# Attention heads with values stationary in column halves, and two head pairs' work interleaved

## What is computed

```python
s = einsum('bqhd,bkhd->bhqk', qn, k_nope) + einsum('bqhr,bkr->bhqk', qp, k_pe)
p = softmax(s.astype(float32) * scale, axis=-1)
o = einsum('bhqk,bkhd->bqhd', p, v)          # then o @ wo
```

## Time and profile before

| | |
|---|---|
| three runs | 3949.35, 3950.53 (median), 3956.2 us |
| profiled execution | span 3955.7 us; the page gives no other time for it |
| TensorE busy | 3625.6 us (92%), mean granted clock 0.956 |
| VectorE, ScalarE, GpSimd busy | 2466.1 (62%), 938.1 (24%), 1840.3 us (47%) |
| chain that ended last | TensorE 71%, VectorE 16%, issue 3%, ScalarE 3% |

### The profile page before, as it was taken

How to read it: one execution, slowest core, us unless ns; L and a number is a source line. 1 busy time by engine, 2 the same in 40 slices (tenths; PEclk the granted TensorE clock), 3 DMA queues, 4 the chain that set the end, 5 groups by cost and what they waited for, 6 DMA issues and landing times.

```text
span 3955.7 us, 74569 instructions
## 1 busy us (share of the span) xinstructions
PE 3625.6 (92%) x31532; PEld 3412.5 (86%) x31532; DVE 2466.1 (62%) x3517; ACT 938.1 (24%) x1804; POOL 1840.3 (47%) x875
## 2 busy tenths in 40 slices
PE   8999999999889778888999994899999989999998
PEld 3877799999788678888999994799998777899997
DVE  5366678758785466655885768886676566632125
ACT  5322231001244255532310012310013222220011
POOL 1311156665455646535566552466554101356663
PEclk9999999999999888889999997899999999999999
DMA  8200024333235543322343331243332000122221
GB/s 318 62 12 17 17 81 147 136 112 123 70 127 182 149 87 94 84 55 102 114 142 119 124 101 36 90 145 128 123 102 73 27 12 17 43 70 75 76 76 53
DMA packets 226844, 367.60 MB, mean 93 GB/s; under 512 B 104752, under 2 KB 111088, under 8 KB 226416
## 3 DMA queue, kind: packets, MB, share of 16 engines
q1 hardware_dynamic: 171408, 255.08, 20.9%
q10 hardware_dynamic: 55136, 107.98, 7.9%
HBM read 326.47 MB, written 36.54 MB: 92 GB/s over the span
## 4 chain that ended last, share of the span: by engine, by line
PE 71%; DVE 16%; issue 3%; ACT 3%; DMA 1%; SPq 1%; POOL 1%; ACTq 1%; DVEq 0%; POOLq 0%
PE ps L819 52%; PE ps L1091 3%; PE ps L1067 3%; DVE f_acc L2159 2%; PE ps L862 2%; PE ps L1077 2%; DVE m_mx L2390 1%; PE ps L1046 1%; DVE r_t L2456 1%; DVE x L2257 1%; DVE r_hlo L2440 1%; DVE ps L2605 1%; PE ps L1027 1%; DVE x L2266 1%; PE ps L879 1%
## 5 line engine op out<-in xcount | busy, mean ns | idle before, releaser
L674 POOL TENSOR_TENSOR w_hi<-w_raw,zrow 128x1024 fp32r<-128x1024 f32 x354 | 693.7, 1959 | 1783.6 <-PE ps L819 979.9
L676 POOL TENSOR_TENSOR w_lo<-w_raw,w_hi 128x1024 fp32r<-128x1024 f32 x354 | 900.2, 2543 | 27.8
L2159 DVE SCALAR_TENSOR_TENSOR f_acc<-f_unit,silu_c,f_acc 128x512 f32<-128x512 f32 x504 | 631.3, 1293 | 7.6
L819 PE MATMUL ps<-f_hhi,w_hi 128*128 128x320 f32 x2688 | 634.1, 317 | 0.0
L819 PE MATMUL ps<-f_hhi,w_lo 128*128 128x320 f32 x2688 | 613.0, 309 | 0.0
L819 PE MATMUL ps<-f_hlo,w_hi 128*128 128x320 f32 x2688 | 610.8, 308 | 0.0
L819 PEld LDWEIGHTS ps<-f_hlo,w_hi 128*128 128x128 f32 x2688 | 449.6, 188 | 0.0
L819 PEld LDWEIGHTS ps<-f_hhi,w_lo 128*128 128x128 f32 x2688 | 448.9, 188 | 0.0
L819 PEld LDWEIGHTS ps<-f_hhi,w_hi 128*128 128x128 f32 x2688 | 441.2, 188 | 0.0
L819 PE MATMUL ps<-f_ahi,w_hi 128*128 128x320 f32 x1408 | 322.2, 310 | 0.2 <-DVE f_alo L2304 0.2
L819 PE MATMUL ps<-f_alo,w_hi 128*128 128x320 f32 x1408 | 320.9, 309 | 0.0
(11 more groups left out here) (401 smaller groups left out, 6710.4 us busy)
## 6 DMA issues: line engine op xcount, KB each, us to landing
w_raw<-in_w SPq DMA_DIRECT2D x340, 512.0 KB, 3.5
f_unit<-in_ada_w ACTq DMA_DIRECT2D x72, 1024.0 KB, 5.8
ada_ring<-in_ada_w SPq DMA_DIRECT2D x24, 1024.0 KB, 6.6
up_scratch<-r_o ACTq DMA_DIRECT2D x40, 320.0 KB, 3.3
s_LW<-up_scratch SPq DMA_DIRECT2D x16, 320.0 KB, 5.1
s_LA<-up_scratch SPq DMA_DIRECT2D x8, 640.0 KB, 6.6
x<-in_x SPq DMA_DIRECT2D x1, 2560.0 KB, 9.4
x_scratch<-r_o ACTq DMA_DIRECT2D x8, 320.0 KB, 2.2
```

Source lines behind the costliest of these rows:

```text
L674: nc.gpsimd.tensor_tensor(whi[:, slot, :], raw[:, raw_slot, :], zrow[:, 0:1].to_broadcast([P, CH * P]), ALU.add).then_inc(w_hi_done, 1)
L676: nc.gpsimd.tensor_tensor(wlo[:, slot, :], raw[:, raw_slot, :], whi[:, slot, :].bitcast(F32), ALU.subtract).then_inc(w_split, 1)
L819: last = mm(ps[:, 2 * b + h, 0:HT], w, r[:, h * HT:(h + 1) * HT], start=kt == 0 and n < 2, stop=kt == KT - 1 and n >= 4)
L2159: last = stt(acc[:, cd, :], unit[:, k, :], by, acc[:, cd, :], ALU.mult, ALU.add)
```

## The change

The hardware loops become straight code, the stage end after the heads goes, and so do the primed semaphores. The work of a pair is put in another order and in part on other engines:

- Blocks now alternate between the two heads: u = 2 qt + hh.
- Weighted sum for one qt and both heads: values stationary (128 keys x 64), head 0 in array columns 0 to 63, head 1 in 64 to 127, with 128 turned queries moving. The output has channels on partitions, so nothing is transposed at the end.
- The reciprocals of the row sums must be spread over partitions: GpSimd makes diagonals, and TensorE multiplies them by ones, in the same halves, into bank 7. VectorE copies bank 7 out and multiplies bank 6 by it.
- ScalarE copies the 512 turned columns, VectorE the 128; ScalarE also copies the upper half of the keys. GpSimd computes the low part.
- Keys and queries of the next pair are issued ahead of the last two weighted sums of this pair; keys now go to banks 0 and 1, queries to 2 to 5.
- `m.pt` holds two qt of both heads. The projection waits for the heads 0 to 13 first, and for the last two heads at its eighth tile.
- GpSimd's chunk stream is cut: in pair j it splits the chunk of pair j + 2.

```diff
 # TensorE
+                def turn(j, u):
+                    pe.wait_ge(q.pexp, q.at.pexp + BLOCKS * j + u + 1)
+                    if u == 0:
+                        pe.wait_ge(q.q_ev, q.at.q_ev + 2 * j + 2)
+                    else:
+                        pe.wait_ge(q.pta, q.at.pta + 10 * j + min(u, 8) + 1)
+                        pe.wait_ge(q.ptd, q.at.ptd + 9 * j + min(u, 8))
...
+                def weighted(j, qt):
+                    pe.wait_ge(q.pta, q.at.pta + 10 * j + min(2 * qt + 3, 10))
+                    pe.wait_ge(q.ptd, q.at.ptd + 9 * j + min(2 * qt + 2, 9))
+                    if qt == 0 and j:
+                        pe.wait_ge(q.oev, q.at.oev + 2 * j)
+                    elif qt == 4:
+                        pe.wait_ge(q.oev, q.at.oev + 2 * j + 1)
+                    kts = range(5) if qt < 4 else (5,)
+                    cols = slice(qt % 4 * P, qt % 4 * P + P)
+                    for n, kt in enumerate(kts):
+                        for hh in range(2):
+                            last = mm(ps[HALF[hh], 6, cols], m.V[:, kt, j * P + hh * 64:j * P + hh * 64 + 64],
+                                      m.pt[:, (5 * j + qt) % 2, hh, n * P:n * P + P], start=n == 0, stop=n == len(kts) - 1)
+                    for t in {3: range(4), 4: (4,)}.get(qt, ()):
+                        pe.wait_ge(q.diag, q.at.diag + BLOCKS * j + 2 * t + 2)
+                        for hh in range(2):
+                            last = mm(ps[HALF[hh], 7, t % 4 * P:t % 4 * P + P], ones[:, 0:64], m.diag[:, 2 * t + hh, :], start=True, stop=True)
+                    last.then_inc(q.av, 1)
+
+                keys(0)
+                queries(0, 0)
+                scores(0, 0)
+                queries(0, 1)
+                scores(0, 1)
+                for j in range(HEADS // 2):
+                    ahead = j + 1 < HEADS // 2
+                    for u in range(BLOCKS):
+                        turn(j, u)
+                        if u < 8:
+                            scores(j, u + 2)
+                        if u in (2, 4, 6):
+                            weighted(j, u // 2 - 1)
+                    if ahead:
+                        keys(j + 1)
+                        queries(j + 1, 0)
+                    weighted(j, 3)
+                    if ahead:
+                        scores(j + 1, 0)
+                        queries(j + 1, 1)
+                    weighted(j, 4)
+                    if ahead:
+                        scores(j + 1, 1)
 # ScalarE
+                def turned(j, u):
+                    g, n = 5 * j + u // 2, 512 if u < 8 else P
+                    act.wait_ge(q.tr, q.at.tr + BLOCKS * j + u + 1)
+                    if g >= 2:
+                        act.wait_ge(q.av, q.at.av + g - 1)
+                    nc.scalar.copy(m.pt[:, g % 2, u % 2, 0:n], ps[:, 4, 0:n]).then_inc(q.pta, 1)
...
+                for j in range(HEADS // 2):
+                    expanded(j)
+                    if j:
+                        hi_part(j - 1, 0)
+                    exponential(j, 0)
+                    if j:
+                        hi_part(j - 1, 1)
+                    exponential(j, 1)
+                    for u in range(8):
+                        turned(j, u)
+                        exponential(j, u + 2)
+                    turned(j, 8)
 # VectorE
+                def output(j, n):
+                    t0, t1 = ((0, TS), (TS, T))[n]
+                    dve.wait_ge(q.av, q.at.av + 5 * j + 4 + n)
+                    if j:
+                        dve.wait_ge(q.olo, q.at.olo + 2 * j)
+                    ch(cp(m.O[:, t0:t1], ps[:, 7, 0:t1 - t0]))
+                    tt(m.O[:, t0:t1], ps[:, 6, 0:t1 - t0], m.O[:, t0:t1], ALU.mult).then_inc(q.oev, 1)
...
+                    for u in range(8):
+                        turned(j, u)
+                        maximum(j, u + 2)
+                        if u % 2:
+                            reciprocals(j, u // 2)
+                    turned(j, 9)
+                    reciprocals(j, 4)
 # GpSimd
+                for j in range(HEADS // 2):
+                    if j:
+                        lo_part(j - 1)
+                    stream(chunk + j, chunk + j + 1)
+                    for u in range(BLOCKS):
+                        diagonal(j, u)
+                lo_part(HEADS // 2 - 1)
```

More of the change, by code:

```diff
@@ L1034, in mla, with keys @@
                 end()
[L1035 to L1040, removed]
+                def keys(j):
+                    if j:
+                        pe.wait_ge(q.pexp, q.at.pexp + BLOCKS * j - 1)
                     for kt in range(2):
@@ L1050, in mla @@
                     last.then_inc(q.head_mm, 1)
[L1051 to L1076, removed]
+                def queries(j, hh):
+                    if j and hh == 0:
+                        pe.wait_ge(q.pexp, q.at.pexp + BLOCKS * j)
+                    elif j:
+                        pe.wait_ge(q.pta, q.at.pta + 10 * j)
+                        pe.wait_ge(q.ptd, q.at.ptd + 9 * j)
+                    panel(3, lambda k: m.qhi[:, k, :], lambda k: m.qlo[:, k, :], 1 + hh).then_inc(q.head_mm, 1)
@@ new lines, in scores @@
+                def scores(j, u):
+                    qt, hh = divmod(u, 2)
+                    if u == 0:
+                        pe.wait_ge(q.q_ev, q.at.q_ev + 2 * j + 1)
+                        pe.wait_ge(q.pta, q.at.pta + 10 * j + 1)
+                    elif u == 1:
+                        pe.wait_ge(q.q_ev, q.at.q_ev + 2 * j + 2)
+                    b, query = 2 * hh, m.Q[:, hh, qt * P:(qt + 1) * P]
+                    if qt == 4:
+                        last = mm(ps[:, b, 0:P], query, m.K[:, hh, T:T + P], start=True, stop=True)
+                    else:
+                        for h in range(2):
+                            last = mm(ps[:, b + h, 0:HT], query, m.K[:, hh, h * HT:(h + 1) * HT], start=True, stop=True)
+                    last.then_inc(q.sc, 1)
@@ L1095, in mla @@
[L1095 to L1105, removed]
@@ L1672, in mla @@
                 end()
[L1673 to L1689, removed]
@@ new lines, in reciprocals @@
+                def reciprocals(j, qt):
+                    dve.wait_ge(q.pexp, q.at.pexp + BLOCKS * j + 2 * qt + 2)
+                    nc.vector.reciprocal(m.rc[:, 2 * qt:2 * qt + 2], m.total[:, 2 * qt:2 * qt + 2]).then_inc(q.rec, 1)
+                for j in range(HEADS // 2):
+                    expanded(j)
+                    queries(j, 0)
+                    if j:
+                        output(j - 1, 0)
+                    maximum(j, 0)
+                    queries(j, 1)
+                    if j:
+                        output(j - 1, 1)
+                    maximum(j, 1)
+                    for u in range(8):
[5 more added lines that the diff above has]
+                    reciprocals(j, 4)
```

157 lines of the change are left out of this document (81 added, 76 removed).

## The result

Median 3863.01 us (3859.27 to 3867.97, four runs) against 3949.94 (3945.2 to 3956.2, four runs) on the same chip: ratio 0.978, 95% interval 0.9766 to 0.9794. The forecast was 3873, the range 3850 to 3905. The profiled execution took 3864.58 us, its span is 3862.1.

The account below looks back on a forecast made before the run. TensorE's order was taken to bound the heads stage of layers 0 and 3. From span 3955.7, stages -75.8 and projection -1.2 gave 3878.7; less 5.2, 3873 us, range 3850 to 3905.

Parts of the forecast that it names:

- Column halves beside each other, 0.224 a key block: Weighted sums on TensorE: both heads' halves run in parallel, 1.12 us for a block pair instead of 2.12.
- rival A: Weighted sums: halves run in series, 0.427 us a key block, 35.5 a pair, 3941 us in all; chance 9%.
- The walk: TensorE's new order in the heads stage, followed through its waits: stalls 3.4 us, pair 31.4, stage 254.5.
- The 0.5 a pair on top: Heads stage: 0.5 us added to each pair because walks come out short, raising the stage from 254.5 to 258.5.
- Clock, 3.4 us in each stage: Heads stage: two falls to the lower clock, half of each lost, 3.4 us; another 1.7 a layer at the projection.
- Tail: Projection's start: VectorE's last evictions and scaling of x take about 10 us, beside 14 us of its first two panels.
- Edits at nothing: Work moved to other engines costs no time: per pair of 31 us, ScalarE 14, VectorE 14, GpSimd under 11.
- D: Rival on ScalarE: function tables swapped at each copy, 1.28 us, 18 times a pair, over 4040 us; chance 1%.
- B: Rival: clock stays low from turn(7) to the fourth sum's end in each pair, slower at 3994 us; chance 4%.
- C: Rival: hand-overs in the pairs longer than walked, 1.2 or 2 us more a pair, 3893 or 3905 us; chance 9%.

Follow-up runs that it names:

- e2: Changed kernel with each weighted sum issuing all key blocks of head 0, then all of head 1, instead of alternating: 3900.16 us, ratio 0.9865.
- e3: Changed kernel with both heads' values as one 128x128 stationary, no column halves, one head after the other: 3911.21 us, ratio 0.9897.
- e1: Kernel before with its heads stage loops written out as straight code, nothing else changed: 3947.04 us, ratio 0.9986.
- e4: Changed kernel with the next pair's keys and queries issued after both last weighted sums instead of ahead of them: 3914.68 us, ratio 0.9905.
- e9: Changed kernel with the eight scalings of x moved from layer 0's projection into its pairs, one in each: 3857.88 us, ratio 0.9767.

## Why the prediction was right

**Column halves beside each other, 0.224 a key block**: right. Of 1.24 for a block pair (1.31 taken) ten steps of 0.107 leave 0.17 for both switches, 0.2 taken. The rows 7 of quarter and corner tiles were the right evidence; rival A would have shown 2.1, and e2 and e3 show what it costs. The measured step is 0.109, so a key block of both heads is 0.218 and not 0.224, which 0.107 did not give either. What I had not seen is that the parallel run hangs on the order of issue.

**The walk**: right, place by place. By starts, scores(1) stands 0.40 (0.43 walked), turn(1) 1.10 (1.16), turn(7) 0.60 (0.70), turn(8) 0.66 (0.61), turn(9) 0.46 (0.52): 3.22 against 3.4. Pair 31.57 against 31.4, first 30.46 against 30.3, last 36.11 against 35.8, its wait 1.61 as said. The stage of 254.5 came out at 255.98.

**The 0.5 a pair on top**: wrong, 4 us a layer of which 1.5 was needed. It was taken from how far the present order's walk fell short, 0.9 a pair; the new order's walk fell short by 0.2. Presumably the rest went with the hand-overs at the pair's end.

**Clock, 3.4 us in each stage**: wrong, none came. With the term above this makes 11.8 us too much for the two stages. The projections were put 2.2 too low (1.2 gained, where the two together lost 1.0), and the 6.9 that the profiled spans differ by outside stages and projections, scatter for the most part, weren't in the sum: 11.8 - 2.2 + 6.9 is, but for rounding, the 16.6 by which the span was over-estimated. Against the median only the first two count, and the forecast was 10 us too high; 3863 lies near the 3858 that the prediction gave for no falls and no added 0.5. The cause of the falls is not settled: e1 keeps them without the loops, e4 has a thinner pair's end and none.

**Tail, "about 10 us beside 14 us"**: wrong. The scaling alone took VectorE 15.7 us from 440.76, as its scalings were held by GpSimd, whose chunks I had costed at nothing here ("nobody waits"). TensorE stood 3.27, and the 1.7 of clock came behind that stand instead of at the projection's start. e9 shows the 5 us. In the total this loss is hidden behind the larger errors of the other sign above.

**Edits at nothing**: ScalarE's copies and GpSimd's diagonals fit: 14.0 us of ScalarE and 9.5 of GpSimd in a pair, where 14 and under 11 were said (VectorE 15.5, where 14 was). The groups for them, stage of layer 0 for ScalarE, the whole kernel for GpSimd:

```profile
L1752 ACT COPY m_PT<-ps 128x512 f32<-128x512 f32 (+1 forms) x72 | 39.2, 544 | 4.2 <-PE ps L1118 4.1
...
L1745 ACT ACT_TABLE_LOAD x1 | 1.3, 1283 | 0.0
```
```profile
L800 POOL TENSOR_TENSOR m_diag<-cst,m_rc 128x128 f32<-128x128 f32 x160 | 60.8, 401 | 212.5 <-DVE m_rc L2484 212.5
```

0.401 us a diagonal (under 0.5 said), one table load a stage, so D is out. (Its price was wrong as well: with ScalarE at 37 us a pair as the bound, the sum comes to some 3955, not to over 4040.) B and C did not come. Straight code brought no stands of its own.

Where the 87 us came from, by single reversals: the halves 36 with one head after the other and 50 at full width, the order 48 (all by the stages), the loops 5. These overlap, so they need not add up. None of e2, e3 and e4 brings the falls of the clock back, so which part of the change ended them is not shown. Nor did a run put the scaling and the turning of the output back where they were.

## What to carry to other kernels

Walk the new order of the bounding engine by starts, with every round trip; where its durations come from rows the sum holds within 1%, and a surcharge taken from the old order's shortfall only spoils it. Follow each piece of work that was moved off the stage to where it now runs: GpSimd's chunks, cut from the stage, cost 5 us in the next one through VectorE. And look for the next independent block to lay over the last stands of a loop's body: twelve keys matmuls moved by one step gave 16 us.

## What the runs showed of the hardware

- Two 128x64 weights in the two column halves, 128 moving columns each: twenty passes in 1.14 to 1.24 us when consecutive instructions alternate, 1.95 when ten follow ten in one half, 2.24 for 128x128 weights. In the 1.95 the second half's stream begins while three passes of the first are still to start, and the two overlap for 0.33 us.
- VectorE scaling a 128x640 tile from and to SBUF beside a busy GpSimd: 15.74 us for eight, 1.97 each, about one for each GpSimd instruction of 2.1 to 2.5 us. Two of them with GpSimd idle, in the kernel before (timeline of VectorE):

```profile
482.98 0.89 DVE L2174 TENSOR_SCALAR x<-x 128x640 f32<-128x640 f32 x2
```

Beside the rows of both kernels in the first section, this shows a hold for a whole instruction of the other engine: the scaling that starts at 444.45 in the changed kernel, beside the split of 444.25 to 446.78, is 2.69 us long. The Trainium skill's "SBUF — State Buffer" (Who interferes with whom) gives the rule, that VectorE's two-port modes and GpSimd lock each other out for a whole instruction; this trace agrees. VectorE's maxima, read from PSUM, were not held: in the changed kernel one takes 0.82 us at 324.20, beside a split that ran from 322.49 to 326.81, and 0.82 at 326.94, away from it.

- The clock fell behind a pair's end with TensorE busy 2.31 of 3.5 us, and did not with 1.89 of 3.5; it fell behind a stand of 1.86 us at the stage's end and did not behind one of 1.61. Which work ahead of a stand holds the clock is open.
- In straight code a table load of 1.28 us stands on the first exponential's path if ScalarE has nothing ahead of it; the changed kernel's follows its copy of the keys (187.39) and has ended 3.8 us before the first exponential.
